# Moving a third of the taps of a depthwise convolution, and the low weight halves, from VectorE to ScalarE and GpSimd

## Chip, cores and metric
The kernel runs on one core of a Trainium2 chip, with all engines of that core: TensorE (PE), VectorE (DVE), ScalarE (ACT), GpSimd (POOL) and the DMA queue of SyncE (SP). The metric is the device time of one execution in microseconds. Inputs are float32, 512 tokens of width 1024.

## The reference
Two pre-norm residual layers. The even layer has a Conformer convolution beside differential attention, the odd layer a gated DeltaNet beside forgetting attention; each is followed by a SwiGLU block, and the end is an RMSNorm. The part that matters here is the even mixer:

```python
def even_mixer(h, ...):
    a_val, a_gate, q, k, v = _split(h @ w_in, [CONV_CH, CONV_CH, DIFF_QK, DIFF_QK, DIFF_V])
    u = a_val * jax.nn.sigmoid(a_gate)
    u = causal_depthwise_conv(u, conv_w) + conv_b   # 31 taps, 512 channels
    u = jax.nn.silu(layer_norm(u, ln_w, ln_b))
    q = partial_rotary(q...); k = partial_rotary(k...)
    o = diff_attention(q, k, v, lam)
    o = rms_norm(o, subln_w) * (1.0 - lambda_init)
    return jnp.concatenate([u, o.reshape(B_, S, DIFF_V)], axis=-1)
```

## The kernel before
Activations are held transposed: channels on the 128 partitions, 512 tokens along the free axis. A float32 product is made of three f32r products of a high and a low half, so each weight tile (128 x 1024 float32, 512 KB) takes this way: SP loads it into one of two buffers `raw`; ACT writes its high half (`hi(t)`, L544) and another engine the rest, raw minus high (`lo(t)`), into one of four slots of `wring`; PE uses it (24 matmuls) and sets `tile_used`. SP loads tile t+2 when hi(t) and lo(t) are done; hi(t) and lo(t) wait until tile t-4 has been used. In the even mixer `lo` is DVE's (L881). POOL has a `lo` of its own (L455), which it uses in the output projections and in the odd mixer.

The order of the even mixer is written out by hand in `even_order()`; each engine walks the same list and takes its own items:

- `val_gate` c = 0 to 3: two weight tiles each (0 to 7). DVE evacuates value and gate (L971), ACT takes the sigmoid, DVE writes the gated chunk c of 128 channels to `upad` (L974).
- `v` 0 to 3: tiles 8 to 11. `v_evac` copies the four values out (L1023).
- `qk`, eight query/key tiles (12 to 19), each in four parts, between which PE does other items. `qk_evac` is DVE's evacuation (L1026), `rope` the rotary product on PE and three DVE instructions (L985 to L988).
- 16 units of differential attention (head, block of 128 queries): `diff_s` scores on PE, `diff_m` maximum on DVE (L994) and exponentials on ACT (L609), `diff_w` combination on DVE (L1000 to L1005), `diff_t` transposes on PE and copy on ACT. The first five units are interleaved with query/key tiles 3 to 7.
- From unit 8 on the layer norm of the convolution (`ln_...`), which begins with POOL adding the four chunks.

The convolution is done tap by tap on DVE: for each of the four chunks one tensor_scalar (L946, tap 0 with the bias) and 30 scalar_tensor_tensor (L949), `cacc = upad shifted x weight + cacc`. They are put between the other DVE items by `pump(n)`, which issues the next n taps, in turns over the first two unfinished chunks that are there: 2 and `TAPS_VAL` in each val_gate, `TAPS_V` after each v, `TAPS_QK` after query/key tiles 0 and 2, one before each `rope`, `TAPS_UNIT` in each of the first five units.

The odd mixer has a short convolution of four taps over 12 chunks, on DVE: one tensor_scalar (L1117) and three scalar_tensor_tensor (L1119) for each chunk, while POOL writes low weight halves (L455).

## Time and profile before
| | |
|---|---|
| three runs, median (lowest, highest) | 1451.31 us (1448.43, 1455.08) |
| the profiled execution: its time, its span | 1448.43 us, 1446.6 us |
| PE, DVE, ACT, POOL busy, of the span | 1328.6, 724.4, 478.5, 174.3 us (92%, 50%, 33%, 12%) |
| L949, the fused taps | 120 instructions, 82.8 us |

Busy time of an engine is the time in which one of its instructions ran; an instruction that is held up after its start is counted as busy. The chain of waits is followed back from the last instruction: at each step to what released it, or to the instruction before it on its engine. A row of the timeline merges neighbours of one kind (x9 is nine of them) and gives in brackets how long the engine had been idle before and what ended that.

### The profile page before, as it was taken

The numbers are of one execution on the slowest core, as the hardware profiler recorded it, in microseconds if no ns is written. First come the engines' busy times: TensorE is split into PE (matmuls) and PEld (weight loads), VectorE is DVE, ScalarE is ACT, GpSimd is POOL, SyncE is SP. The second block draws the span as 40 slices with busy tenths as digits, with TensorE's granted clock in tenths as the row PEclk, the third lists the DMA queues.
The fourth block names the chain that finished last, engine by engine and source line by source line (L and its number), as shares of the span: only waits on it lengthen the run. The fifth ranks groups of instructions, "written<-read, shape, count | busy, mean of one in ns | idle before, by whom it ended". The sixth has DMA issues, their size and how long they took to land.

```text
span 1446.6 us, 16892 instructions
## 1 busy us (share of the span) xinstructions
PE 1328.6 (92%) x6250; PEld 1080.9 (75%) x6250; DVE 724.4 (50%) x991; ACT 478.5 (33%) x693; POOL 174.3 (12%) x103
## 2 busy tenths in 40 slices
PE   6886777899999999998998999987999999999995
PEld 4664445788888888886886888875788888888884
DVE  5898874454544442227874315355454544442223
ACT  4221234543333332214344322444343333332211
POOL 3000011410000000002423233210410000000005
PEclk9997887999999999999999999999999999999997
DMA  5221100123232232331221111100123232232221
GB/s 187 86 79 54 44 29 1 48 83 103 87 109 94 87 106 98 101 101 59 88 73 44 59 58 44 59 1 0 46 85 103 87 109 94 87 106 97 101 72 58
DMA packets 30718, 109.60 MB, mean 76 GB/s; under 512 B 3410, under 2 KB 3666, under 8 KB 30674
## 3 DMA queue, kind: packets, MB, share of 16 engines
q1 hardware_dynamic: 30674, 108.99, 22.5%
q8 instruction: 31, 0.51, 0.1%
q14 instruction: 13, 0.11, 0.0%
HBM read 106.88 MB, written 2.10 MB: 75 GB/s over the span
## 4 chain that ended last, share of the span: by engine, by line
PE 78%; DVE 16%; ACT 3%; issue 2%; POOL 1%; DMA 0%; DVEq 0%; SPq 0%; POOLq 0%; ACTq 0%
PE PS L1273 76%; DVE cacc L949 5%; DVE wring L881 2%; DVE hbuf L824 1%; DVE hbuf L1119 1%; ACT wring L544 1%; PE PS L1607 1%; DVE amax L994 1%; DVE HH L828 1%; POOL ssq L469 1%; PE PS L1349 0%; ACT pbuf L609 0%; DVE xT L842 0%; DVE qk L988 0%; DVE outT L1267 0%
## 5 line engine op out<-in xcount | busy, mean ns | idle before, releaser
L1273 PE MATMUL PS<-HH,wring 128*128 128x512 f32 x3096 | 747.5, 400 | 21.4 <-DVE wring L881 12.1
L1273 PEld LDWEIGHTS PS<-HH,wring 128*128 128x128 f32 x3096 | 585.8, 192 | 151.4 <-issue 20.9
L1273 PE MATMUL PS<-AA,wring 128*128 (+1 forms) x1440 | 328.2, 390 | 4.4 <-DVE AA L1010 2.8
L1273 PEld LDWEIGHTS PS<-AA,wring 128*128 128x128 f32 x1440 | 269.9, 188 | 61.9 <-DVE AA L1010 3.6
L852 DVE TENSOR_TENSOR ubuf<-PS,rstd 128x512 f32<-128x512 f32 x44 | 30.4, 691 | 198.1 <-PE PS L1273 198.1
L455 POOL TENSOR_TENSOR wring<-raw,wring 128x1024 fp32r<-128x1024 f32 x37 | 93.1, 2519 | 283.7 <-ACT wring L544 280.8
L874 DVE TENSOR_TENSOR wring<-raw,wring 128x1024 fp32r<-128x1024 f32 x36 | 44.1, 1226 | 149.6 <-ACT wring L589 149.6
L544 ACT ACTIVATE wring<-raw 128x1024 fp32r<-128x1024 f32 x73 | 76.7, 1053 | 122.7 <-PE PS L1273 81.2
L861 DVE TENSOR_TENSOR wring<-raw,wring 128x1024 fp32r<-128x1024 f32 x88 | 107.5, 1222 | 0.9 <-ACT wring L581 0.4
L466 POOL TENSOR_TENSOR ssq<-sqb 128x512 f32<-128x512 f32 x5 | 7.9, 1576 | 712.4 <-ACT sqb L557 712.4
L576 ACT ACTIVATE AA<-ubuf 128x512 f32 x44 | 27.9, 633 | 198.2 <-DVE ubuf L859 198.2
L581 ACT ACTIVATE wring<-raw 128x1024 fp32r<-128x1024 f32 x88 | 92.0, 1045 | 1.1 <-DMA raw<-w_stream 1.1
L589 ACT ACTIVATE wring<-raw 128x1024 fp32r<-128x1024 f32 x36 | 38.2, 1061 | 155.5 <-PE PS L1273 152.0
L949 DVE SCALAR_TENSOR_TENSOR cacc<-upad,vec,cacc 128x512 f32<-128x512 f32 x120 | 82.8, 745 | 0.5
L734 ACT ACTIVATE G<-PS 128x512 f32<-128x512 f32 x60 | 35.7, 595 | 105.2 <-PE PS L1607 52.7
L570 ACT ACTIVATE gbuf<-gbuf 128x512 f32<-128x512 f32 x44 | 27.8, 632 | 108.4 <-DVE gbuf L852 108.4
L1273 PE MATMUL PS<-wring,HH 128*128 128x512 f32 x192 | 51.2, 416 | 6.1 <-DVE hbuf L971 6.0
L881 DVE TENSOR_TENSOR wring<-raw,wring 128x1024 fp32r<-128x1024 f32 x36 | 45.5, 1278 | 20.9 <-ACT wring L544 20.8
L842 DVE TENSOR_TENSOR xT<-xT,PS 128x512 f32<-128x512 f32 x32 | 21.9, 683 | 59.5 <-PE PS L1273 59.5
L852 DVE TENSOR_TENSOR gbuf<-PS,rstd 128x512 f32<-128x512 f32 x44 | 30.4, 691 | 38.5 <-PE PS L1273 38.1
L1177 DVE COPY_PREDICATED G<-consts,PS 128x512 f32<-128x512 int32 x24 | 17.8, 741 | 63.6 <-PE PS L1273 63.6
L1273 PEld LDWEIGHTS PS<-wring,HH 128*128 128x128 f32 x192 | 36.8, 199 | 14.1 <-DVE hbuf L971 6.5
(232 smaller groups left out, 1132.7 us busy)
## 6 DMA issues: line engine op xcount, KB each, us to landing
raw<-w_stream SPq DMA_DIRECT2D x197, 512.0 KB, 3.2
xT<-x_t SPq DMA_DIRECT2D x4, 512.0 KB, 6.1
out_t<-outT SPq DMA_DIRECT2D x8, 256.0 KB, 2.1
rope<-rope_const SPq DMA_DIRECT2D x1, 576.0 KB, 4.4
consts<-shape_const SPq DMA_DIRECT2D x1, 576.0 KB, 5.8
consts<-shape_const SPq DMA_DIRECT2D x1, 192.0 KB, 7.0
vec<-vectors SPq DMA_DIRECT2D x1, 115.0 KB, 2.0
rowv<-row SPq DMA_DIRECT2D x1, 0.0 KB
```

The source lines that it names most:

```text
L455: nc.gpsimd.tensor_tensor(wring[:, t % RING, 1], raw[:, t % RAW], wring[:, t % RING, 0].bitcast(f32), ALU.subtract).then_inc(lo_ready[t % ...
L544: nc.scalar.activation(wring[:, t % RING, 0], raw[:, t % RAW], ACT.Copy).then_inc(hi_ready[t % RING], 1)
L576: nc.scalar.activation(AA[:, bass.ds(r * 2 + c, 1), 0].rearrange("p a b -> p (a b)"), ubuf[:, c], ACT.Copy).then_inc(sem("ffn_hi"), 1)
L581: nc.scalar.activation(wring[:, t % RING, 0], raw[:, t % RAW], ACT.Copy).then_inc(hi_ready[t % RING], 1)
L589: nc.scalar.activation(wring[:, t % RING, 0], raw[:, t % RAW], ACT.Copy).then_inc(hi_ready[t % RING], 1)
L734: nc.scalar.activation(out, hd(bank), func, **kw).then_inc(gdn_act[st], 1)
L852: V.tensor_tensor(buf[:, c], PS[:, 2 * c + u], rstd[:], ALU.mult).then_inc(evacuated, 1)
L861: V.tensor_tensor(wring[:, t % RING, 1], raw[:, t % RAW], wring[:, t % RING, 0].bitcast(f32), ALU.subtract).then_inc(lo_ready[t % RING], 1)
L874: V.tensor_tensor(wring[:, t % RING, 1], raw[:, t % RAW], wring[:, t % RING, 0].bitcast(f32), ALU.subtract).then_inc(lo_ready[t % RING], 1)
L881: V.tensor_tensor(wring[:, t % RING, 1], raw[:, t % RAW], wring[:, t % RING, 0].bitcast(f32), ALU.subtract).then_inc(lo_ready[t % RING], 1)
L949: ins = V.scalar_tensor_tensor(cacc[:, c], upad[:, c, k:k + S], vcol(V_CONVW + TAPS * c + k), cacc[:, c], ALU.mult, ALU.add)
L1273: return nc.tensor.matmul(out, lhsT, rhs, start=start, stop=stop)
```

## The change
1. Of the 124 taps, 39 leave DVE: taps 0 to 7 of chunk 2 and all 31 of chunk 3. ACT multiplies the shifted chunk by the weight into a ring `prod` of eight buffers (tap 0 of each goes with its bias straight to `cacc`), and POOL adds `prod` to `cacc`. They are a new item, `shared_taps`, two after each `v` and four after part 1 of each query/key tile. Semaphores `tap_product` (ACT to POOL) and `conv_added` (POOL to itself, to ACT for the ring, to DVE ahead of its tap 8 of chunk 2, and to POOL's first addition of the layer norm) go with it.
2. The low halves of tiles 4 to 23 (20 of them), written by DVE in `val_gate`, `v` and `qk_evac`, are written by POOL at the same items.
3. DVE's taps are fewer per item: 6, 5, 4, 5, 4 in place of 9, 8, 7, 7, 6.

```diff
--- before.py
+++ after.py
@@ -68,7 +68,10 @@
 OUT_DVE = 5
 
 
-TAPS_VAL, TAPS_V, TAPS_QK, TAPS_UNIT, TAPS_LATE = 9, 8, 7, 7, 6
+SHARED = 8
+PROD = 8
+POOL_TAPS_V, POOL_TAPS = 2, 4
+TAPS_VAL, TAPS_V, TAPS_QK, TAPS_UNIT, TAPS_LATE = 6, 5, 4, 5, 4
 LN_FROM = 8
 LAG = 6
 FILL_STEPS = 75
@@ -136,7 +139,16 @@
                      ("sub_lo", 0), ("sub_lo", 1), ("sub_lo", 2), ("conv_silu", 0), ("sub_mul", 3)]
     order += [("conv_lo", c) for c in range(4)] + [("sub_hi", 3), ("sub_lo", 3)]
 
-    return [item for item in order if item]
+    out, m = [], 0
+    for item in order:
+        if item:
+            out.append(item)
+            n = POOL_TAPS_V if item[0] == "v" else POOL_TAPS if item[0] == "qk" and item[1][1] == 1 else 0
+            if n and m < SHARED + TAPS:
+                out.append(("shared_taps", (m, min(m + n, SHARED + TAPS))))
+                m = min(m + n, SHARED + TAPS)
+    assert m == SHARED + TAPS
+    return out
 
 
 def fox_order():
@@ -302,7 +314,7 @@
     pbuf, q = at("pbuf", [2, 2, S], f32, q)
     wbuf, q = at("wbuf", [2, S], f32, q)
     assert q <= at_A + 4 * 2 * S * 4
-    prod, _ = at("prod", [2, S], f32, at_A + 4 * 2 * S * 4)
+    prod, _ = at("prod", [PROD, S], f32, at_A + 4 * 2 * S * 4)
     q = at_H
     oT, q = at("oT", [H, S], f32, q)
     osq, q = at("osq", [H, S], f32, q)
@@ -361,6 +373,14 @@
 
     def vcol(n):
         return vec[:, n:n + 1]
+
+    def shared_tap(m):
+
+        return (2, m) if m < SHARED else (3, m - SHARED)
+
+    def added(m):
+
+        return m if m < SHARED else m - 1
 
     sems = {}
 
@@ -472,10 +492,29 @@
             add_squares(0, n)
         nc.gpsimd.memset(upad[:, :, 0:TAPS - 1], 0.0).then_inc(sem("pad_zero"), 1)
 
+        def add_taps(m0, m1):
+            for m in range(m0, m1):
+                c, k = shared_tap(m)
+                if k:
+                    pool.wait_ge(sem("tap_product"), m + 1)
+                    if k > 1:
+                        pool.wait_ge(sem("conv_added"), added(m) - 1)
+                    nc.gpsimd.tensor_tensor(cacc[:, c], cacc[:, c], prod[:, m % PROD], ALU.add).then_inc(sem("conv_added"), 1)
+
         for kind, a in even_order():
-            if kind == "ln_add":
-
-                pool.wait_ge(sem("conv_done"), 4)
+            if kind == "val_gate":
+                lo(2 * a + RING)
+                lo(2 * a + 1 + RING)
+            elif kind == "v":
+                lo(8 + a + RING)
+            elif kind == "qk_evac":
+                lo(12 + a + RING)
+            elif kind == "shared_taps":
+                add_taps(*a)
+            elif kind == "ln_add":
+
+                pool.wait_ge(sem("conv_done"), 3)
+                pool.wait_ge(sem("conv_added"), added(SHARED + TAPS - 1))
                 for c in range(1, 4):
                     if c > 1:
                         pool.wait_ge(sem("ln_chunks"), c - 1)
@@ -620,11 +659,28 @@
                                  PS[:, bank, 0:(i + 1) * P].rearrange("p (j c) -> p j c", c=P),
                                  ACT.Copy).then_inc(sem(sem_c), 1)
 
+        def multiply_taps(m0, m1):
+
+            for m in range(m0, m1):
+                c, k = shared_tap(m)
+                if k == 0:
+                    act.wait_ge(sem("gated"), c - 1)
+                if m > PROD:
+                    act.wait_ge(sem("conv_added"), added(m - PROD))
+                w = vcol(V_CONVW + TAPS * c + k)
+                if k == 0:
+                    ins = nc.scalar.activation(cacc[:, c], upad[:, c, 0:S], ACT.Identity, bias=vcol(V_CONVB + c), scale=w)
+                else:
+                    ins = nc.scalar.activation(prod[:, m % PROD], upad[:, c, k:k + S], ACT.Copy, scale=w)
+                ins.then_inc(sem("tap_product"), 1)
+
         for kind, a in even_order():
             if kind == "qk" and a == (0, 0):
                 act.wait_ge(sem("masks_loaded"), 16)
                 nc.scalar.activation(mask16[:, 0], ident, ACT.Copy).then_inc(sem("mask16"), 1)
                 nc.scalar.activation(mask16[:, 1], cmask, ACT.Copy).then_inc(sem("mask16"), 1)
+            if kind == "shared_taps":
+                multiply_taps(*a)
             if kind == "val_gate":
                 hi(2 * a + RING)
                 hi(2 * a + 1 + RING)
@@ -931,10 +987,10 @@
         def taps():
 
 
-            tap, count = [0] * 4, [0] * 4
+            tap, count = [0, 0, SHARED], [0] * 3
             turn = 0
             while True:
-                open_ = [c for c in range(gated[0]) if tap[c] < TAPS][:2]
+                open_ = [c for c in range(min(gated[0], 3)) if tap[c] < TAPS][:2]
                 if not open_:
                     yield False
                     continue
@@ -945,7 +1001,10 @@
                 if k == 0:
                     ins = V.tensor_scalar(cacc[:, c], upad[:, c, 0:S], vcol(V_CONVW + TAPS * c), vcol(V_CONVB + c), ALU.mult, ALU.add)
                 else:
-                    dve.wait_ge(dchain, count[c])
+                    if count[c]:
+                        dve.wait_ge(dchain, count[c])
+                    else:
+                        dve.wait_ge(sem("conv_added"), added(SHARED - 1))
                     ins = V.scalar_tensor_tensor(cacc[:, c], upad[:, c, k:k + S], vcol(V_CONVW + TAPS * c + k), cacc[:, c],
                                                  ALU.mult, ALU.add)
                 if k < TAPS - 1:
@@ -971,10 +1030,12 @@
                 V.tensor_tensor(buf[:, c % 2], PS[:, (2 * c + m) % 4], rstd[:], ALU.mult).then_inc(evacuated, 1)
             pump(2 if c else 0)
             dve.wait_ge(sem("gate_sig"), c + 1)
-            link(V.tensor_tensor(upad[:, c, TAPS - 1:], hbuf[:, c % 2], sqb[:, c % 2], ALU.mult))
+            ins = V.tensor_tensor(upad[:, c, TAPS - 1:], hbuf[:, c % 2], sqb[:, c % 2], ALU.mult)
+            if c < 2:
+                link(ins)
+            else:
+                ins.then_inc(sem("gated"), 1)
             gated[0] += 1
-            lo(2 * c + RING)
-            lo(2 * c + 1 + RING)
             pump(TAPS_VAL)
 
         def rope_finish(j):
@@ -1015,8 +1076,6 @@
                 val_gate(a)
             elif kind == "taps":
                 pump(a)
-            elif kind == "v":
-                lo(8 + a + RING)
             elif kind == "v_evac":
                 dve.wait_ge(tile_used, 12)
                 for b in range(NB):
@@ -1025,7 +1084,6 @@
                 dve.wait_ge(tile_used, 12 + a + 1)
                 V.scalar_tensor_tensor(hbuf[:, a % 2], PS[:, QK_BANK[a]], 1.0 if a % 2 else SC_DIFF, rstd[:],
                                        ALU.mult, ALU.mult).then_inc(evacuated, 1)
-                lo(12 + a + RING)
             elif kind == "rope":
                 rope_finish(a)
             elif kind == "diff_m":
```

## Rows read from the trace of the kernel before

**Rows 1.** Windows: length; busy of PE, PEld, DVE, ACT, POOL; PEclk; DMA share, GB/s.
```profile
42.00:76.00 34.00, 26.19 (x111) 20.52 (x110) 33.44 (x47) 7.75 (x9) 0.00 (x0) 0.98 0.28 93
76.00:115.00 39.00, 29.77 (x120) 24.04 (x119) 38.97 (x57) 6.34 (x8) 0.00 (x0) 0.85 0.24 81
115.00:132.00 17.00, 15.18 (x58) 10.36 (x59) 13.66 (x20) 3.62 (x8) 0.00 (x0) 0.88 0.18 63
132.00:198.00 66.00, 48.31 (x172) 30.91 (x171) 56.57 (x92) 12.71 (x33) 2.68 (x3) 0.84 0.12 40
```

**Rows 2.** Chain of waits, 42 to 198 us: by line; a piece (start, us).
```profile
by line: DVE cacc L949 49.4%; DVE wring L881 13.6%; PE PS L1273 6.8%; issue 4.5%; DVE amax L994 3.0%; ACT pbuf L609 2.7%; DVE qk L988 2.7%; ACT wring L544 2.5%; DVE qk L985 2.4%; DVE sqb L986 2.4%; DVE upad L974 1.8%; DVE vtk L1023 1.7%; DV
...
80.39 5.96 DVE cacc L949 x9
```

**Rows 3.** Groups of the vector engine, 42 to 198 us: busy, mean, idle.
```profile
L949 DVE SCALAR_TENSOR_TENSOR cacc<-upad,vec,cacc 128x512 f32<-128x512 f32 x120 | 82.8, 745 | 0.5
L881 DVE TENSOR_TENSOR wring<-raw,wring 128x1024 fp32r<-128x1024 f32 x19 | 22.9, 1220 | 6.9 <-ACT wring L544 6.8
L1026 DVE SCALAR_TENSOR_TENSOR hbuf<-PS,rstd 128x512 f32<-128x512 f32 x8 | 5.5, 683 | 1.2 <-PE PS L1273 1.2
...
L986 DVE TENSOR_TENSOR sqb<-PS,rope 128x512 f32<-128x512 f32 x7 | 4.8, 683 | 0.0
...
L946 DVE TENSOR_SCALAR cacc<-upad,vec 128x512 f32<-128x512 f32 x4 | 2.2, 538 | 0.0
```

**Rows 4.** Timeline of PE: start, us, idle before it and releaser.
```profile
75.52 5.06 PE L1273 MATMUL PS<-wring,HH 128*128 128x512 f32 x11 [6.02 <-DVE hbuf L971]
...
115.06 2.04 PE L1273 MATMUL PS<-hbuf,rope 128*128 128x512 f32 x2 [9.30 <-DVE hbuf L1026]
```

**Rows 5.** Line L1026: min/median/max ns, first and last start.
```profile
L1026 DVE SCALAR_TENSOR_TENSOR hbuf<-PS,rstd x8: 674/681/692, 114.2 to 197.5; 128x512 f32<-128x512 f32 x8
```

**Rows 6.** Timeline of the vector engine, 691 to 765 us, the short convolution.
```profile
691.30 2.33 DVE L1119 SCALAR_TENSOR_TENSOR hbuf<-cin,vec,hbuf 128x512 f32<-128x512 f32 x3
...
694.98 4.34 DVE L1119 SCALAR_TENSOR_TENSOR hbuf<-cin,vec,hbuf 128x512 f32<-128x512 f32 x3
...
759.85 4.47 DVE L1119 SCALAR_TENSOR_TENSOR hbuf<-cin,vec,hbuf 128x512 f32<-128x512 f32 x3
```

**Rows 7.** Timeline of GpSimd in four places.
```profile
195.17 1.27 POOL L482 TENSOR_TENSOR prod<-cacc 128x512 f32<-128x512 f32 x1 [171.52 <-DVE cacc L949]
...
273.17 4.95 POOL L455 TENSOR_TENSOR wring<-raw,wring 128x1024 fp32r<-128x1024 f32 x2 [49.76 <-ACT wring L544]
...
307.77 1.62 POOL L469 TENSOR_TENSOR ssq<-ssq,sqb 128x512 f32<-128x512 f32 x1 [3.82 <-ACT sqb L557]
...
695.98 2.79 POOL L455 TENSOR_TENSOR wring<-raw,wring 128x1024 fp32r<-128x1024 f32 x1 [6.16 <-ACT wring L544]
```

**Rows 8.** Timeline of the vector engine beside GpSimd in three other places.
```profile
13.27 0.49 DVE L824 TENSOR_SCALAR hbuf<-xT,vec 128x512 f32<-128x512 f32 x1
...
14.46 1.32 DVE L824 TENSOR_SCALAR hbuf<-xT,vec 128x512 f32<-128x512 f32 x1
...
273.09 0.68 DVE L842 TENSOR_TENSOR xT<-xT,PS 128x512 f32<-128x512 f32 x1
273.81 2.05 DVE L824 TENSOR_SCALAR hbuf<-xT,vec 128x512 f32<-128x512 f32 x1
...
306.41 0.69 DVE L828 TENSOR_TENSOR HH<-hbuf,HH 128x512 fp32r<-128x512 f32 x1
307.01 1.22 DVE L881 TENSOR_TENSOR wring<-raw,wring 128x1024 fp32r<-128x1024 f32 x1
308.15 1.78 DVE L828 TENSOR_TENSOR HH<-hbuf,HH 128x512 fp32r<-128x512 f32 x1
```

**Rows 9.** Tile cacc: an activation, min/median/max ns.
```profile
L656 ACT ACTIVATE ytmp<-cacc,vec x4: 800/800/817, 259.2 to 261.4; 128x512 f32<-128x512 f32 x4
```

**Rows 10.** Groups of the scalar engine, 42 to 198 us.
```profile
L544 ACT ACTIVATE wring<-raw 128x1024 fp32r<-128x1024 f32 x17 | 18.0, 1059 | 61.3 <-PE PS L1273 35.1 <-DMA raw<-w_stream 26.2
```

## Prediction

> **What bounds the kernel now.** I read the page first, for the span and the engines, then the stretches around the convolution, the chain of waits, the groups of the vector engine, and last the timeline wherever the vector engine and GpSimd work at the same time. The profiled execution took 1448.43 us, with a span of 1446.6. All that the change touches lies between 42 us, where the first gated channel chunk is written, and 198 us, where the last query/key tile is evacuated. There the vector engine (DVE) is busy 33.4 + 39.0 + 13.7 + 56.6 = 142.6 us of 156, and TensorE (PE) 26.2 + 29.8 + 15.2 + 48.3 = 119.4 us [rows 1]. From 76 to 115 us DVE has no free time at all, and the chain of waits gives half of the stretch to the taps (L949) and another 14% to the lo halves (L881) [rows 2]. PE pays for it: it stands 6.0 us for the evacuation of the last value/gate tile and 9.3 us for that of the first query tile [rows 4]. GpSimd (POOL) does nothing before 132 us, ScalarE (ACT) is busy a fifth of the time [rows 1]. So this stretch is bound by DVE in program order, and what lengthens or shortens DVE's work here moves the end almost one to one. What comes after 198 us is the same in both kernels, and I let it move with the stretch.
>
> **What goes from DVE.** Chunk 2 loses its first 8 taps and chunk 3 all 31: two of these are plain tensor_scalar, 37 the fused form. In a row of taps one starts every 5.96 / 9 = 0.66 us [rows 2] (its 745 ns overlap the next [rows 3]), so this is 37 x 0.66 + 2 x 0.46 (538 ns [rows 3] less the same 0.08 of overlap) = 25.4 us. The 20 lo halves of tiles 4 to 23 leave too: 20 x 1.14 (1220 ns less 0.08 [rows 3]) = 22.8 us. Together 48.2 us. If nothing were paid for it, DVE would need 94.4 us of the stretch and PE's 119.4 would bound it.
>
> **What ACT gets.** 39 multiplications with a scale from a vector. The nearest row, an ACTIVATE of the same size with scale and bias from vectors, is 800 ns [rows 9]; the bare one of twice the size takes 1059 [rows 10]. So 39 x 0.6 to 0.8 = 23 to 31 us, on an engine with 156 - 30.4 us free [rows 1]. In its order they sit after a hi conversion and ahead of the transposed copy and the exponentials of a unit, 4 at a time: 2.4 to 3.2 us, in time in which ACT waits for DVE's maximum. I take nothing for them. Without that cover each of the eight groups would cost up to 3 us, 24 in all; the product ring of 8 also lets ACT wait for POOL's additions of two groups before, which comes to the same.
>
> **What POOL gets.** 37 additions (taps 1 to 7 and 1 to 30) at 1.27 us each, as its only one of this form beside an idle DVE [rows 7], 47 us, and 20 lo halves at about 2.4 (the two at 273 us took 4.95 [rows 7]), 48 us: 95 us of 156. By itself that fits, and the four-slot ring of weights leaves a tile's lo half three tiles of PE work (over 15 us) before PE asks for it. DMAs: none is added, but SP's load of tile t+2 waits for lo(t), which now stands behind up to 4 additions in POOL's queue (about 5 us). With a DMA share of 0.24 or less from 76 us on [rows 1] I take nothing for it. Two waits are new to DVE and to the chunk's order: its tap 8 of chunk 2 waits for POOL's seven additions, with the rotary work queued behind it. DVE comes to that tap only after 56 others, in the query/key tiles, and POOL's seven are in the value tiles before; I take nothing, and a microsecond or two if POOL is late.
>
> **What POOL's work costs DVE.** This is the term that decides. Later in the same kernel DVE runs exactly this fused form, three in a chain. Undisturbed the three take 2.33 us; with one lo half on POOL beside them they take 4.34 [rows 6, 7]. Of the twelve such triples between 691 and 768 us nine are of the long kind; the last of these took 4.47 [rows 6]. So one lo half stops DVE for 2.0 to 2.2 us. With an addition on POOL a DVE subtraction of two SBUF operands grows from 0.69 to 1.78 us [rows 8]: 1.1 us; a tensor_scalar grew from 0.49 to 1.32, 0.83 us [rows 8]. That subtraction stood right behind another DVE instruction, and POOL, waiting since 307.77, still got in between [rows 7, 8]: where both have work, they take turns. A DVE instruction that takes one operand from PSUM kept its 0.68 us at 273.09 beside POOL's lo half, while the tensor_scalar after it grew to 2.05, by 1.6 [rows 8]. So evacuations, PSUM products and maxima run beside POOL; taps, the gated product, two thirds of the rotary work and the combinations do not. The Trainium skill (SBUF — State Buffer, "Who interferes with whom") has this as an exclusive lock between the two engines, held for the whole instruction. The rows agree in kind. By a whole instruction of POOL's the sum below would be 12 us higher (95 us in place of 83); the growth in the rows is smaller, and I go by the rows.
>
> Full price: 20 x 2.1 + 37 x 1.1 = 82.7 us on DVE against 48.2 saved, so +34.5 us if nothing of it is covered. Cover is DVE's idle time, 156 - 142.6 = 13.4 us, and its instructions that read PSUM: two groups of 5.5 and 4.8 us [rows 3], ten other evacuations of the same size (7) and seven maxima (an estimate of 5), some 22 us. With all of it used: 34.5 - 35.4 = -1. With the cheapest growth seen (0.83 us for an addition, 1.6 for a lo half) and all cover, 62.6 - 48.2 - 35.4 = -21. I walk through the stages to see how much cover is really met:
>
> - 42 to 76 us: 9 taps and 6 lo halves go (6.0 + 6.8 = 12.8 us); lo halves 4 to 11 come on POOL, 8 x 2.1 = 16.8, of which some 3 fall beside the wait for the sigmoid and the evacuations. +1. PE's wait of 6.0 us stays.
> - 76 us to the first query evacuation at 114.2 [rows 5]: 15 taps and 6 lo halves go (16.7 us). DVE has 28 taps in a row and POOL has always something ready (lo 12 to 16, and ACT and POOL run ahead of PE with chunk 2's seven additions and seven of chunk 3), so they take turns: 5 x 2.1 + 14 x 1.1 = 25.9. +9. PE's wait of 9.3 us grows to 18.
> - 115 to 132 us: two tiles, DVE partly idle; one lo half and four additions fall beside the rotary work. +2 (0 to 5).
> - 132 to 198 us: five more lo halves and 19 additions, 10.5 + 20.9 = 31.4; 12 taps and 5 lo halves go, 13.6; of the 17.8 left, 9.4 is met by DVE's idle time in this stage (66 - 56.6 [rows 1]; 6.8 of the idle in the whole stretch was DVE waiting for ACT ahead of its own lo halves [rows 3], which falls away) and some 2 by PSUM instructions, since the additions come right behind a lo half, when DVE has rotary work and taps, and not when it has its maxima. +6. The last of the eight evacuations, at 197.5 now [rows 5], comes near 216.
>
> Sum: 1 + 9 + 2 + 6 = +18 us; 1448.4 + 18 = 1466.4. The three runs have a median of 1451.3, 3 us above the profiled one; I forecast 1467.
>
> **The rivals.**
> - POOL's work is hidden and DVE's 48 us are gained. For it: POOL idle until 132 us [rows 1], DVE busy 91% of the stretch. Then PE's 119.4 us bound the stretch, 36.6 us less, 1412 us; half hidden, about 1430. Against it: nine of twelve triples. It decides from the point where less than 48 of the 83 us fall into time that DVE needs; by my count it is 67.
> - A draw: the growths are the small ones and most PSUM instructions are met, 62.6 - 48.2 - 13.4 = +1, 1444 to 1456.
> - PE becomes the second loser: longer waits let its granted clock fall. From 76 to 115 us, with the waits, it was 0.85, at 132 to 198 0.84, against 0.98 before 76 [rows 1]; at 1.2 GHz a tile of 24 products is twice as long. If the five units lose another 2 to 3 us each, that is +10 to 15 on top, 1477 to 1485.
> - ACT in the way: its groups of multiplications delay exponentials, up to 24 us more, the same place in the range.
>
> **How the numbers follow.** Under 0.5% (7 us) a measurement of this kernel can't tell from no change. The stall of DVE with the clock as now (1456 to 1477): 0.50. With PE or ACT on top (1477 to 1495): 0.16. A draw: 0.14. Hidden: 0.20. So slower 0.66, same 0.14, faster 0.20. The likeliest case alone spans 1456 to 1477; the range that leaves out 2 in 10 goes from 1440 to 1488.
>
> **What would show it.** Right: fused taps of 745 ns with a share at 1.8 (an addition) and 2.9 us (a lo half), a mean well over 1 us; DVE's busy time in the stretch as long as before or longer although its instructions are 59 fewer; the first query evacuation near 124 us and not before 115; the last well after 198; PE's wait before the first rotary product longer than 9.3 us. ACT's multiplications near 0.7 us with no waits behind them. Wrong: taps of 745 ns throughout; the last query/key evacuation before 198 us; a chain of waits that leads from 42 to 198 us mainly over PE; or POOL waiting in DVE's stead, its additions at 1.9 us and DVE's undisturbed.

## The result, and the profile after

The changed kernel took 1462.54 us (median of ten runs, 1458.36 to 1468.19), the kernel before 1451.71 us on the same chips (ten runs, 1448.16 to 1455.73). The ratio is 1.007, with a 95% interval of 1.005 to 1.0091: slower, by 10.8 us. The profiled execution took 1462.84 us, with a span of 1459.7.

The stretches of the changed kernel, with the columns of [rows 1]:

```profile
42.00:76.00 34.00, 24.87 (x110) 20.27 (x108) 33.57 (x30) 7.29 (x9) 18.13 (x7) 0.93 0.36 124
76.00:115.00 39.00, 36.20 (x146) 29.04 (x146) 28.79 (x39) 15.60 (x23) 30.27 (x11) 0.93 0.13 44
115.00:132.00 17.00, 7.54 (x27) 4.47 (x28) 12.25 (x11) 6.54 (x12) 16.28 (x10) 0.60 0.16 55
132.00:198.00 66.00, 43.25 (x155) 28.41 (x154) 63.95 (x71) 21.65 (x46) 41.50 (x25) 0.81 0.12 40
```

VectorE (DVE) issues 151 instructions here, 65 fewer than in [rows 1] (59 by the change; the rest lies in the slower order, which has not come as far by 198 us), and is busy 138.6 us where it had been busy 142.6. So the instructions left take longer. But the stages differ from the forecast: from 76 to 115 us TensorE (PE) is busy 36.2 us, 6.4 more than before, and DVE is idle for 10.2 us; from 115 to 132 us PE works 7.5 us where it had worked 15.2. Something was gained and given back. The groups by line, 42 to 198 us, say what grew:

```profile
L1008 DVE SCALAR_TENSOR_TENSOR cacc<-upad,vec,cacc 128x512 f32<-128x512 f32 x83 | 88.6, 1111 | 5.4 <-POOL cacc L502 4.9
...
L475 POOL TENSOR_TENSOR wring<-raw,wring 128x1024 fp32r<-128x1024 f32 x17 | 55.5, 3274 | 41.0 <-ACT wring L583 41.0
L502 POOL TENSOR_TENSOR cacc<-cacc,prod 128x512 f32<-128x512 f32 x34 | 51.6, 1519 | 3.3
...
L674 ACT ACTIVATE prod<-upad,vec 128x512 f32<-128x512 f32 x35 | 23.0, 712 | 3.2 <-POOL cacc L502 3.2
```

The 83 fused taps on DVE (L1008) take 88.6 us; 120 took 82.8 before [rows 3]. GpSimd's (POOL's) low halves (L475) average 3.27 us, though one takes 2.4 to 2.5 undisturbed. And there is a wait that was not there, 4.9 us of DVE for POOL's additions (L502). The evacuations of the query tiles, to be held against [rows 5]:

```profile
L1085 DVE SCALAR_TENSOR_TENSOR hbuf<-PS,rstd x8: 673/680/692, 104.9 to 204.9; 128x512 f32<-128x512 f32 x8
```

The first comes 9.4 us earlier than before, the last 7.4 us later. The timeline of DVE shows where that turns:

```profile
78.72 17.30 DVE L1008 SCALAR_TENSOR_TENSOR cacc<-upad,vec,cacc 128x512 f32<-128x512 f32 x26
99.42 2.73 DVE L1082 TENSOR_SCALAR vtk<-PS,rtok 128x512 f32<-128x512 f32 x4 [3.39 <-PE PS L1331]
104.86 0.69 DVE L1085 SCALAR_TENSOR_TENSOR hbuf<-PS,rstd 128x512 f32<-128x512 f32 x1 [2.71 <-PE PS L1331]
105.47 5.43 DVE L1008 SCALAR_TENSOR_TENSOR cacc<-upad,vec,cacc 128x512 f32<-128x512 f32 x3
115.80 3.42 DVE L1008 SCALAR_TENSOR_TENSOR cacc<-upad,vec,cacc 128x512 f32<-128x512 f32 x2 [4.91 <-POOL cacc L502]
119.14 1.75 DVE L1046 TENSOR_TENSOR qk<-hbuf,rope 128x512 f32<-128x512 f32 x1
120.81 0.68 DVE L1047 TENSOR_TENSOR sqb<-PS,rope 128x512 f32<-128x512 f32 x1
121.52 2.12 DVE L1049 TENSOR_TENSOR qk<-qk,sqb 128x512 f32<-128x512 f32 x1
123.56 0.68 DVE L1085 SCALAR_TENSOR_TENSOR hbuf<-PS,rstd 128x512 f32<-128x512 f32 x1
```

And that of POOL beside it:

```profile
84.30 13.98 POOL L475 TENSOR_TENSOR wring<-raw,wring 128x1024 fp32r<-128x1024 f32 x1 [11.82 <-ACT wring L583]
98.25 1.28 POOL L502 TENSOR_TENSOR cacc<-cacc,prod 128x512 f32<-128x512 f32 x1
...
106.88 3.46 POOL L502 TENSOR_TENSOR cacc<-cacc,prod 128x512 f32<-128x512 f32 x2
110.30 2.83 POOL L475 TENSOR_TENSOR wring<-raw,wring 128x1024 fp32r<-128x1024 f32 x1
113.10 7.23 POOL L502 TENSOR_TENSOR cacc<-cacc,prod 128x512 f32<-128x512 f32 x5
```

From 78.72 to 96.02 us DVE runs 26 taps without a hold-up, 0.66 us each. POOL's low half, begun at 84.30, ends at 98.28, 2.26 us after the last of those taps: it did its work only when DVE had stopped. No turns were taken. The additions, whose products ACT had written from 85 us on, began at 98.25. DVE came to the ninth tap of chunk 2, its own first there, at 110.9, found them unfinished and stood 4.91 us; now turns were taken, and the five taps around it took 8.85 us where undisturbed ones take 3.3. Between the first two evacuations lie 18.7 us; it had been 9.0. PE stood for 11.86 us of it, before the rotary product of the second query tile:

```profile
106.02 1.02 PE L1331 MATMUL PS<-hbuf,rope 128*128 128x512 f32 x2
106.48 6.05 PE L1331 MATMUL PS<-HH,wring 128*128 128x512 f32 x24
124.39 2.05 PE L1331 MATMUL PS<-hbuf,rope 128*128 128x512 f32 x2 [11.86 <-DVE hbuf L1085]
```

It is the successor of the 9.30 us in [rows 4], one tile later.

### The profile page after: what moved, and what is told of

It is laid out like the page before. It is cut to its first block, busy times and chain, and to the rows that moved or that the text cites. A ratio compares the mean times of both kernels' runs of the same rounds, so it can differ in the third digit from the quotient of the medians.

```text
span 1459.7 us, 16982 instructions
## 1 busy us (share of the span) xinstructions
PE 1332.5 (91%) x6250; PEld 1085.1 (74%) x6250; DVE 728.7 (50%) x932; ACT 502.3 (34%) x732; POOL 293.3 (20%) x160
## 3 DMA queue, kind: packets, MB, share of 16 engines
q1 hardware_dynamic: 30674, 108.99, 21.6%
## 4 chain that ended last, share of the span: by engine, by line
PE 79%; DVE 13%; issue 3%; ACT 2%; POOL 2%; DMA 0%; DVEq 0%; SPq 0%; POOLq 0%; ACTq 0%
PE PS L1331 78%; DVE cacc L1008 4%; DVE hbuf L880 1%; DVE qk L1046 1%; PE PS L1665 1%; POOL cacc L502 1%; DVE HH L884 1%; DVE amax L1055 1%; PE PS L1407 1%; POOL ssq L489 1%; DVE qk L1049 1%; DVE hbuf L1177 0%; ACT wring L583 0%; DMA xT<-x_t 0%; DVE xT L898 0%
## 5 line engine op out<-in xcount | busy, mean ns | idle before, releaser
L1331 PE MATMUL PS<-HH,wring 128*128 128x512 f32 x3096 | 746.4, 399 | 20.1 <-DVE wring L937 12.2
L475 POOL TENSOR_TENSOR wring<-raw,wring 128x1024 fp32r<-128x1024 f32 x57 | 155.8, 2739 | 352.8 <-ACT wring L583 352.8
L930 DVE TENSOR_TENSOR wring<-raw,wring 128x1024 fp32r<-128x1024 f32 x36 | 44.1, 1226 | 149.6 <-ACT wring L628 149.6
L917 DVE TENSOR_TENSOR wring<-raw,wring 128x1024 fp32r<-128x1024 f32 x88 | 107.5, 1221 | 0.9 <-ACT wring L620 0.4
L583 ACT ACTIVATE wring<-raw 128x1024 fp32r<-128x1024 f32 x73 | 76.4, 1052 | 84.3 <-PE PS L1331 54.2
L1008 DVE SCALAR_TENSOR_TENSOR cacc<-upad,vec,cacc 128x512 f32<-128x512 f32 x83 | 88.6, 1111 | 5.4 <-POOL cacc L502 4.9
L502 POOL TENSOR_TENSOR cacc<-cacc,prod 128x512 f32<-128x512 f32 x37 | 56.2, 1519 | 3.6
L489 POOL TENSOR_TENSOR ssq<-ssq,sqb 128x512 f32<-128x512 f32 x30 | 42.5, 1415 | 44.0 <-ACT sqb L596 43.0
```

The source lines that it names most:

```text
L475: nc.gpsimd.tensor_tensor(wring[:, t % RING, 1], raw[:, t % RAW], wring[:, t % RING, 0].bitcast(f32), ALU.subtract).then_inc(lo_ready[t % ...
L489: nc.gpsimd.tensor_tensor(ssq[:], ssq[:], sqb[:, n % 2], ALU.add).then_inc(ssq_done, 1)
L502: nc.gpsimd.tensor_tensor(cacc[:, c], cacc[:, c], prod[:, m % PROD], ALU.add).then_inc(sem("conv_added"), 1)
L583: nc.scalar.activation(wring[:, t % RING, 0], raw[:, t % RAW], ACT.Copy).then_inc(hi_ready[t % RING], 1)
L917: V.tensor_tensor(wring[:, t % RING, 1], raw[:, t % RAW], wring[:, t % RING, 0].bitcast(f32), ALU.subtract).then_inc(lo_ready[t % RING], 1)
L930: V.tensor_tensor(wring[:, t % RING, 1], raw[:, t % RAW], wring[:, t % RING, 0].bitcast(f32), ALU.subtract).then_inc(lo_ready[t % RING], 1)
```

## The experiments

The questions were four: is it the contention between DVE and POOL that eats the 48 us, or the new order with its waits; which of the two kinds of work on POOL costs what; what kept POOL out for 14 us; and can DVE be taken out of the contention. All kernels below start from the changed kernel, except where another is named.

**Both kinds of POOL's work made small (pool_small).** Instructions, waits and semaphores stay, but POOL's subtraction and addition touch 16 columns only, so the output lacks most of the low parts of the weights of tiles 4 to 23 and most of 37 taps. `lo_small` stands for `lo` in `val_gate`, `v` and `qk_evac`; "..." marks lines left out.

```diff
+        def lo_small(t):
+            ...
+            nc.gpsimd.tensor_tensor(wring[:, t % RING, 1, 0:16], raw[:, t % RAW, 0:16], wring[:, t % RING, 0, 0:16].bitcast(f32), ALU.subtract)
-                    nc.gpsimd.tensor_tensor(cacc[:, c], cacc[:, c], prod[:, m % PROD], ALU.add)
+                    nc.gpsimd.tensor_tensor(cacc[:, c, 0:16], cacc[:, c, 0:16], prod[:, m % PROD, 0:16], ALU.add)
```

> The changed kernel, but POOL's 37 additions and its 20 low halves of the even mixer work on 16 columns only (the rest of the sums and of the low halves is left out); every item, wait and order stays. Theory A (POOL's work costs DVE through the port that both use): the 48 us that left DVE are now really gained and PE bounds the stretch, 1412 to 1425 us. Rival B (what is lost lies in the order, in ACT's multiplications or in PE's own waits): the time stays near the changed kernel's, above 1445.

Measured: 1412.76 us (1405.49 to 1416.46), ratio 0.9715 (0.9677 to 0.9754). The taps are undisturbed, and the last query evacuation comes at 155.0:

```profile
L1016 DVE SCALAR_TENSOR_TENSOR cacc<-upad,vec,cacc x83: 741/746/781, 45.0 to 149.2; 128x512 f32<-128x512 f32 x83
```

So with the order and all waits as changed, the kernel is 39 us faster than before if POOL's instructions are short, and the length of POOL's instructions costs 49.8 us. The order, ACT's 39 products and the waits are not what makes it slow.

**One kind made small at a time (adds_small, lo_small).** In the first, only the additions touch 16 columns (37 taps are mostly missing from the output), in the second only the low halves (the low weight parts are mostly missing).

> The changed kernel with only the 37 additions cut to 16 columns (most of the sums is left out), the low halves whole. Theory A: DVE gets back up to 37 x 1.1 us less what was covered, and the wait for the seven additions goes; fused taps stay long only beside low halves; 1425 to 1442 us. If the low halves alone made the loss: above 1450.

> The changed kernel with only the 20 low halves on POOL cut to 16 columns (most of each is left out), the additions whole. With adds_small at 1438.5 and both cut at 1412.8: if the two prices simply add up, the low halves cost 26 us and the additions 24, and this takes 1436 to 1440. If POOL's additions come mainly late because the low half before them waits (theory C), it takes less, 1420 to 1432.

Measured: additions small 1438.53 us (1434.72 to 1443.85), ratio 0.9921 (0.9892 to 0.995); low halves small 1432.3 us (1424.16 to 1436.15), ratio 0.9849 (0.9809 to 0.9889). Against 1462.5 the additions cost 24.0 us and the low halves 30.2. The two nearly add up to the 49.8 (54.2); the expectation for the second had 1436 to 1440 us for prices that simply add and 1420 to 1432 for additions that come late behind a waiting low half, and 1432.3 lies on the edge of the latter and decides little. Per instruction that is 0.65 us of the kernel's time for an addition and 1.5 for a low half.

**One part of the change at a time (taps_only, lo_only).** First the taps only, with the low halves back on DVE; then, made from the kernel before, the low halves only, with all 124 taps on DVE. Of each edit one engine's part is shown; the other engine gains or loses the same `lo` items.

```diff
 taps only, POOL:
-            if kind == "val_gate":
-                lo(2 * a + RING)
-            ...
 low halves only, DVE of the kernel before:
-            lo(2 * c + RING)
-            lo(2 * c + 1 + RING)
```

> Part 1 alone: taps shared with ACT and POOL, low halves back on DVE. Theory A (price per addition 1.1 us wherever DVE has a gap): 25 us leave DVE, up to 41 come back, some 13 of them covered: 1446 to 1460. Theory C (the loss is that POOL comes late, since its first low half waited 12 us for a run of taps and the additions behind it): without low halves POOL isn't late, 1428 to 1440.

> Part 2 alone: the 20 low halves on POOL, all 124 taps on DVE with the old counts. Theory A: 23 us leave DVE, 20 x 2.1 = 42 come back less what is covered; 1450 to 1465. Theory C: DVE runs 41 taps without a gap from about 78 us; POOL gets none of its low halves in before 105 us and PE waits for tile 12 for some 8 us, with fused taps at 745 ns in that run; the same range, told apart by the length of the first low half after 80 us (over 15 us by C, under 4 by A with turns).

Measured: taps only 1466.14 us (1465.14 to 1467.19), ratio 1.0101 (1.0083 to 1.012); low halves only 1468.6 us (1465.29 to 1474.15), ratio 1.0128 (1.0101 to 1.0155). Each half of the change alone is as slow as both together or slower, and slower than any theory on record had it (6 us above 1460, 4 above 1465): less of the price is covered than was estimated. With the taps only, DVE's low halves cut its taps into fives, and POOL takes its turns from 79 us on. The first row is of DVE, the second of POOL:

```profile
93.30 8.51 DVE L1001 SCALAR_TENSOR_TENSOR cacc<-upad,vec,cacc 128x512 f32<-128x512 f32 x5
```
```profile
92.04 16.43 POOL L502 TENSOR_TENSOR cacc<-cacc,prod 128x512 f32<-128x512 f32 x9 [2.33 <-ACT prod L667]
```

Five taps in 8.51 us are 1.70 each, 1.04 above the undisturbed 0.66. With the low halves only, the first query evacuation comes at 125.5; the first low half after 80 us took 8.9 us, between the "over 15" and "under 4" of the two theories.

**Without the wait for seven additions (chunk3).** `SHARED = 0`: POOL and ACT take chunk 3 alone, and chunk 2 is all DVE's, so DVE waits for none of POOL's additions (DVE has 8 taps more, POOL 7 additions fewer).

> The changed kernel, but only chunk 3 is shared (31 taps on ACT and POOL, 93 on DVE), so that DVE never waits for POOL's additions. DVE has 8 taps more (5.3 us), POOL 7 additions less (7.7 us of price, most of it uncovered), and the wait of 4.9 us goes. Theory C (lateness costs): 1452 to 1458, 5 us or more under the changed kernel. Theory A (only the price on the port): 1459 to 1463.

Measured: 1464.0 us (1462.03 to 1470.35), ratio 1.009 (1.0063 to 1.0117). The second query evacuation comes at 118.38, 5.2 us earlier than in the changed kernel, but the fourth at 152.69 beside 152.54, and the last at 202.9. So the wait's 4.9 us aren't what the kernel loses by: the theory that made the wait the cause expected 1452 to 1458 us, and is out (the other had 1459 to 1463, 1 us too low). The lock-out is here as well: a low half took 14.34 us from 83.96 us on. That the 8 taps more on DVE, in the units, are what gave the 5 us back is the likely reading, not a shown one.

**Gaps between the taps (one_chunk).** DVE takes its taps from one chunk at a time, so that each waits for the one before it. With that its own taps cost more, about 0.79 us each.

```diff
-                open_ = [c for c in range(min(gated[0], 3)) if tap[c] < TAPS][:2]
+                open_ = [c for c in range(min(gated[0], 3)) if tap[c] < TAPS][:1]
```

> The changed kernel, but DVE does the taps of one chunk after another and not of two in turns, so that every tap waits for the one before it. Theory D (POOL gets the port only when DVE leaves a gap or POOL held it last): the first low half after 80 us takes under 4 us and not 14, POOL's seven additions are done in time, and DVE's wait for them (4.9 us) goes, but in the value tiles DVE is held up as the prediction had it; the taps start 0.79 us apart at best. 1465 to 1485 us. Rival (the run of taps isn't what kept POOL out): the low half keeps its 14 us.

Measured: 1474.29 us (1469.36 to 1475.29), ratio 1.0149 (1.0132 to 1.0166). POOL first, then DVE:

```profile
88.37 2.45 POOL L475 TENSOR_TENSOR wring<-raw,wring 128x1024 fp32r<-128x1024 f32 x1 [12.14 <-ACT wring L583]
90.78 1.47 POOL L502 TENSOR_TENSOR cacc<-cacc,prod 128x512 f32<-128x512 f32 x1
```
```profile
91.14 32.92 DVE L1008 SCALAR_TENSOR_TENSOR cacc<-upad,vec,cacc 128x512 f32<-128x512 f32 x18
```

The low half that took 13.98 us takes 2.45; DVE pays in its stead, 1.83 us for each of the next 18 taps, and its first query evacuation comes at 126.6. There is no wait for additions any more.

**How long a run keeps POOL out (lo_last, lo_turn3).** Two more, made from low halves only. There the run over chunks 0 and 1 kept POOL out from 90.89 to about 97.4 us, but a later one over chunks 1 and 2, with taps as close, let it in after 0.4 us. The first kernel turns over the last two unfinished chunks once there are four, the second over three chunks in place of two.

```diff
-                open_ = [c for c in range(gated[0]) if tap[c] < TAPS][:2]
+                open_ = [c for c in range(gated[0]) if tap[c] < TAPS]
+                open_ = open_[-2:] if gated[0] == 4 else open_[:2]
 and in the other one:
+                open_ = [c for c in range(gated[0]) if tap[c] < TAPS][:3]
```

> lo_only with one difference: once all four chunks are there (85 us), VectorE takes its taps in turns from the last two unfinished chunks (2 and 3) and not from the first two (0 and 1). Open question: in lo_only a run of taps over chunks 0 and 1 kept GpSimd out from 90.9 to 97.4 us, and the same kind of run over chunks 1 and 2, with starts every 0.66 us too, let it in after 0.4 us. Theory that a run without gaps keeps it out by itself: it stays out here until the run ends or changes its chunks, some 10 us or more, and the first low half of about 90 us takes over 10 us. Theory that it hangs on which buffers the run touches: the low half of about 90 us gets in at once, 2.4 to 2.9 us long, the following ones too, and each stops VectorE for 2.1 us: first query evacuation 124 to 130 us, time 1464 to 1475 us.

> lo_only with turns over three unfinished chunks in place of two, so that the tap on which the next one of its chunk depends is three instructions back. Theory that GpSimd gets in through the small wait of a tap for the one two before it: here there is none, the run keeps GpSimd out wherever three chunks are open (from 70 us on), the low halves of 75 to 120 us take over 8 us each and TensorE waits for them, first query evacuation before 120 us. Theory that the spacing of dependent taps plays no part: the low halves behave as in lo_only (one long wait of 5 to 10 us, then 2.4 to 2.9 us each), first query evacuation 122 to 128 us, time 1462 to 1475 us. In either case the taps start every 0.66 us where GpSimd is quiet.

Measured: last two 1470.23 us (1466.98 to 1473.55), ratio 1.0117 (1.0092 to 1.0142); three in turns 1463.31 us (1462.97 to 1467.74), ratio 1.0069 (1.0053 to 1.0086). Of the first kernel, DVE and then POOL:

```profile
87.99 25.92 DVE L957 SCALAR_TENSOR_TENSOR cacc<-upad,vec,cacc 128x512 f32<-128x512 f32 x39
113.83 2.72 DVE L1027 TENSOR_SCALAR vtk<-PS,rtok 128x512 f32<-128x512 f32 x4
124.17 0.69 DVE L1030 SCALAR_TENSOR_TENSOR hbuf<-PS,rstd 128x512 f32<-128x512 f32 x1 [7.62 <-PE PS L1276]
```
```profile
92.78 25.66 POOL L455 TENSOR_TENSOR wring<-raw,wring 128x1024 fp32r<-128x1024 f32 x2 [14.06 <-ACT wring L551]
```

39 taps ran at 0.66 us each over chunks 2 and 3, and POOL, with a low half begun at 92.78, got nothing done until they ended: two low halves took 25.66 us. The theory of the buffers, by which chunks 2 and 3 would have let it in at once, is out, though the first evacuation (124.2) and the time lie inside what it had forecast. DVE's taps are now undisturbed, but PE waits 8.4 us for the low half, and DVE waits 7.6 us for PE instead: the time is the same as with turns. With three in turns POOL's pair took 22.63 us from 90.38, and it got in when the first tap of the last chunk, a tensor_scalar at 108.22, cut the run; in low halves only it was such a first tap too, at 97.43. The expectation for it was met in the first, long hold, missed in the low halves after it (2.5 to 2.8 us, not over 8) and by 0.9 us in the evacuation (120.9, not before 120). So POOL gets into a close run of three chunks in turn as well (at 115.17). What sets the entries at 104.37 and 112.66 us of low halves only apart is taken up in the last section.

**DVE's operand taken out of SBUF (psum_acc).** In the changed kernel, the sums of chunks 0 and 1 stay in two idle PSUM banks until their last tap, so each of their taps reads one operand from SBUF and one from PSUM. Chunk 2 begins after both, PE waits for them before the scores that need the banks, and the counts of taps are 7, 6, 4, 4, 4.

```diff
+        def acc(c):
+            return PS[:, 6 + c] if c < 2 else cacc[:, c]
 ...
-                    ins = V.scalar_tensor_tensor(cacc[:, c], upad[:, c, k:k + S], vcol(V_CONVW + TAPS * c + k), cacc[:, c],
+                    ins = V.scalar_tensor_tensor(acc(c) if k < TAPS - 1 else cacc[:, c], upad[:, c, k:k + S], vcol(V_CONVW + TAPS * c + k), acc(c),
 ...
+                if a == 1:
+                    pe.wait_ge(sem("conv_done"), 2)
```

> The changed kernel, but DVE's sums of chunks 0 and 1 stand in PSUM (banks 6 and 7, free until the second scores) up to their last tap, so that 60 of DVE's 83 fused taps read one operand from SBUF and one from PSUM; one chunk pair first, then chunk 2; two taps more per value/gate tile pair, one more per value tile and one less per unit. Theory A (DVE instructions with one SBUF operand run beside POOL): up to 125 us POOL's work costs DVE almost nothing and those taps stay at 0.75 us, the first low half after 80 us takes under 3 us; 1430 to 1442 us, under both kernels. Rival (POOL holds up any DVE instruction, or the taps get longer with PSUM): no gain, 1455 or more.

Measured: 1434.81 us (1431.4 to 1441.02), ratio 0.9883 (0.9851 to 0.9915): 27.7 us less than the changed kernel and 17 less than the one before. It computes the whole reference and beats both. DVE and POOL of the same place:

```profile
70.04 16.54 DVE L1011 SCALAR_TENSOR_TENSOR PS<-upad,vec,PS 128x512 f32<-128x512 f32 x25
```
```profile
72.66 2.40 POOL L475 TENSOR_TENSOR wring<-raw,wring 128x1024 fp32r<-128x1024 f32 x1 [3.09 <-ACT wring L583]
75.02 1.29 POOL L502 TENSOR_TENSOR cacc<-cacc,prod 128x512 f32<-128x512 f32 x1
78.10 2.41 POOL L475 TENSOR_TENSOR wring<-raw,wring 128x1024 fp32r<-128x1024 f32 x1 [1.78 <-ACT wring L583]
80.47 2.73 POOL L502 TENSOR_TENSOR cacc<-cacc,prod 128x512 f32<-128x512 f32 x2
```

25 taps at 0.66 us each, and in the same time low halves at 2.4 and additions at 1.3 us: neither holds up the other. Most of these taps also write to PSUM, so it could be the writing that counts. It isn't: a last tap reads PSUM and writes SBUF, and it kept its 0.73 us in the middle of POOL's additions:

```profile
86.50 0.73 DVE L1011 SCALAR_TENSOR_TENSOR cacc<-upad,vec,PS 128x512 f32<-128x512 f32 x1
85.91 2.73 POOL L502 TENSOR_TENSOR cacc<-cacc,prod 128x512 f32<-128x512 f32 x2
```

The taps and rotary products that still read two operands from SBUF go on paying, in the groups of DVE from 42 to 210 us:

```profile
L1011 DVE SCALAR_TENSOR_TENSOR PS<-upad,vec,PS 128x512 f32<-128x512 f32 x58 | 40.1, 747 | 0.5
L1011 DVE SCALAR_TENSOR_TENSOR cacc<-upad,vec,cacc 128x512 f32<-128x512 f32 x23 | 31.2, 1356 | 0.4
L1049 DVE TENSOR_TENSOR qk<-hbuf,rope 128x512 f32<-128x512 f32 x8 | 15.0, 1877 | 1.8 <-PE PS L1334 1.8
```

**The same sums in PSUM without POOL (psum_before), and with the low halves only (psum_lo).** The edit of the last kernel, made in the kernel before and in low halves only, with their own counts.

> The kernel before, with the sums of chunks 0 and 1 kept in PSUM until their last tap and nothing moved to GpSimd or ScalarE. Contention theory (PSUM sums helped the changed kernel only because a tap with one operand from PSUM runs beside GpSimd): nothing runs on GpSimd here between 42 and 195 us, so nothing is gained: taps 740 to 750 ns, first query evacuation 112 to 116 us, time 1447 to 1456 us, ratio 0.997 to 1.003. Rival (a sum in PSUM is cheaper for VectorE by itself, or shortens its chain of dependent taps): the 62 taps gain 0.1 us or more each, the first query evacuation comes before 109 us, time below 1445 us. Second rival (it is dearer by itself, by the wait that TensorE gets before its second scores): above 1457 us.

> Low halves on GpSimd, all 124 taps on VectorE as in lo_only, with the sums of chunks 0 and 1 in PSUM until their last tap. Contention theory: the low halves that fall beside chunks 0 and 1 (about 10 of 20, until some 95 us) cost VectorE nothing and don't wait for it (1.3 to 2.5 us each, no start later than 3 us after its high half), so 22.8 us leave VectorE and 10 x 2.1 = 21 less idle time and PSUM cover (about 12) come back: 12 to 15 us less than the kernel before on VectorE, first query evacuation 98 to 106 us, time 1436 to 1446 us. Rival (what psum_acc won came from the 39 taps that left VectorE, and low halves on GpSimd cost as much as before): 1460 to 1470 us, as lo_only had 1468.6.

Measured: without POOL 1456.12 us (1450.45 to 1460.42), ratio 1.003 (1.0017 to 1.0043); with low halves 1447.0 us (1445.54 to 1449.55), ratio 0.9966 (0.9953 to 0.9979). Without POOL the sums in PSUM gain nothing and cost 0.3%. A first tap takes 0.81 us there, not 0.54, and chunk 2 begins later; that these make the 0.3% is not shown. (Its first query evacuation, at 119.1, lies outside the 112 to 116 expected, and the time 0.1 us above its 1447 to 1456, but 3.3 of its 4.9 us were there before the first tap: the first gated product began at 45.47 in place of 42.14.) So the gain of the kernels above is the absence of contention and not a cheaper tap. With the low halves it is 21.6 us less than low halves only; the low halves beside the runs in PSUM took 2.35 to 2.6 us, with no hold. The first query evacuation came at 108.7, 3 us later than the latest expected, and the time 1 us above the range given.

## Why the prediction was right, and where it was not

**The outcome and the mechanism** were right: slower, by 10.8 us where 15.7 were forecast (1462.5 for 1467.0), inside the likeliest case's 1456 to 1477. What eats the gain is DVE held up by POOL, which pool_small isolates and psum_acc with psum_before confirms.

**What goes from DVE (48.2 us)** was sized well. From the first gated chunk to the last query/key evacuation, of the kernel before, the changed one and pool_small (columns of [rows 1]):

```profile
42.14:197.55 155.41, 119.31 (x459) 85.69 (x457) 142.18 (x213) 29.86 (x53) 2.31 (x2) 0.88 0.19 65
42.14:204.90 162.76, 118.58 (x459) 86.54 (x457) 144.30 (x154) 53.57 (x92) 112.54 (x55) 0.84 0.18 62
43.69:154.95 111.26, 104.51 (x459) 78.43 (x457) 95.05 (x155) 53.02 (x92) 31.73 (x54) 1.00 0.25 86
```

With POOL's instructions short, DVE is busy 95.0 us (94.4 in the prediction). The hidden rival's 1412 us was met (1412.8), but in part by luck: the granted clock was 1.00, PE was busy 104.5 us and not 119.4, and the stretch got 44 us shorter where 36.6 were counted; by the first addition to the residual it was 37.1 us (234.9 for 272.0).

**The prices** held wherever turns are taken. An addition beside a tap costs 1.04 us (1.1 in the prediction). A rotary product beside a low half takes 2.91 us where it had taken 0.68, so 2.2 (2.0 to 2.2). Of the changed kernel, DVE, then POOL:

```profile
155.02 2.91 DVE L1046 TENSOR_TENSOR qk<-hbuf,rope 128x512 f32<-128x512 f32 x1
```
```profile
154.91 2.47 POOL L475 TENSOR_TENSOR wring<-raw,wring 128x1024 fp32r<-128x1024 f32 x1 [7.03 <-ACT wring L583]
```

One row was used for more than it shows: the instruction with a PSUM operand at 273.09 [rows 8] had begun before POOL's at 273.17 [rows 7], so it could not have been held up. That such instructions do run beside POOL is seen in the changed kernel, whose first query evacuation took 0.69 us at 104.86 inside this low half:

```profile
104.53 2.41 POOL L475 TENSOR_TENSOR wring<-raw,wring 128x1024 fp32r<-128x1024 f32 x1
```

**How much of the price was paid** was mis-sized. The full price was put at 82.7 us and by the walk through the stages about 66 were to be paid (48.2 + 18). DVE paid 49.3 (144.3 less 95.0 busy), and its idle time in the stretch grew by 5.2 (18.5 for 13.2), nearly all of it the wait of 4.9. How the 33 us that were not paid divide into idle time, PSUM reads and the 14 us in which POOL was locked out was not measured.

**The stages** against the sum. Starts of four evacuations, before and after, with the shift of each and the forecast shift up to there:

| | before | after | shift | forecast |
|---|---|---|---|---|
| last value/gate (L971, L1030) | 74.79 | 75.60 | +0.8 | +1 |
| first query (L1026, L1085) | 114.24 | 104.86 | -9.4 | +10 |
| third query/key | 132.24 | 133.59 | +1.4 | +12 |
| last query/key | 197.55 | 204.90 | +7.4 | +18 |

The first stage is right (+0.8 for +1; only PE's wait in it, which was to stay at 6.0 us, was 9.5) and so is the last, 132 to 198 us (+6.0 for +6). **The step that failed** is that of 76 us to the first query evacuation: "DVE has 28 taps in a row and POOL has always something ready [...], so they take turns", 25.9 us, +9. It came out at -10.2. That taps stand in a row is just what kept POOL out: in 17.3 us not one tap was held up. The rows it was read from ([rows 6 to 8]) were a chain of three dependent taps and a subtraction with another instruction ahead; none was a long run without gaps. one_chunk, in which the taps do have gaps, shows what the step described: first query evacuation 126.6 (forecast "near 124"), and 1474 us. Its own taps are slower too, so its 1474 is no clean price of the turns.

**The next step failed with it.** 115 to 132 us was put at +2, and the wait for seven additions at nothing, "a microsecond or two if POOL is late". POOL was late because it had been locked out (in one_chunk, without the lock-out, there is no such wait), and DVE came to the tap after 53 others, not 56. From the first to the third evacuation the shift is +10.7: the second tile alone has 4.9 us of waiting, 5.5 us of hold in five taps and 2.5 in the rotary work, less 3.1 for the low half and three taps that left DVE there. So the two errors, 19 us too dear and 9 too cheap, left the sum 11 us too high at 198 us, and 5 in the end. That the total came out right is in part luck.

**Whether the lock-out itself made the kernel slower** is not shown. chunk3, without the wait, gains nothing in the end; lo_last, with a lock-out nearly twice as long, takes what low halves only takes, and lo_turn3, whose first low half was held for 20.1 us, takes 5 us less. A likely reading, not a shown one: what DVE wins by it PE loses, since PE needs POOL's low halves as much as DVE's evacuations.

**Behind 198 us** I let the work move with the stretch. In the profiled pair, the first addition to the residual comes 9.2 us later (272.0 before, 281.2 after), where 7.4 came in; the one at 906.9 us is 8.3 late. The spans differ by 13.1 us and the medians by 10.8: the 2 to 5 us past the 8 lie within what single runs of one kernel differ by, and no place is named for them.

**The other rivals.** PE's clock: the granted 0.60 of 115 to 132 us stands for a stage in which PE had 7.5 us of work; from 132 to 198 us it was 0.81 against 0.84 [rows 1], and the stage cost no more than forecast. Over the whole stretch PE was busy 118.6 us, and 119.3 before. ACT in the way: its products took 712 ns (forecast 0.6 to 0.8) and waited 3.2 us in all for POOL. Neither came. The Trainium skill (SBUF — State Buffer, "Who interferes with whom") says that the shared ports are an exclusive lock, that the first to issue gets them for its whole instruction (written in that section of VectorE's two-port modes), that issue order decides who blocks, and that a VectorE instruction with at most one SBUF input does not contend. The turns after 98 us and the taps of psum_acc, which read one operand from SBUF and ran free, agree with that page. The hold of 13.98 us does not follow from it, since it spans 18 instructions of DVE and not the one that was under way.

**Of the signs named,** the mean tap of 1111 ns, the taps beside additions and low halves, DVE's busy time as long as before (144.3 us for 142.2, with 59 instructions fewer, up to the last evacuation), the late last evacuation and ACT's 712 ns were there. The first query evacuation was not: at 104.9 it met the sign that was to show the forecast wrong ("not before 115"), and PE's long wait came a tile later. The last evacuation came at 204.9, not 216.

## What to carry to other kernels

Before work is moved from VectorE to GpSimd, count for each VectorE instruction beside it how many operands it reads from SBUF: here the move would have freed 39 us of the kernel's time and contention took 50, and the same move with 60 of the taps reading their running sum from PSUM was worth 17 us. A price of contention read from short chains didn't hold here for a long run of instructions without gaps: there GpSimd was the one that stood, and whoever waited for GpSimd paid later. Follow the work that another engine owes through the whole stage before a new wait is put down at nothing.

## What the runs showed of the hardware that was not expected

A run of VectorE instructions with two SBUF operands each and no gaps (0.66 us apart) kept GpSimd out to its end: 13.98 us beside a run of 26 taps, 25.66 us for two low halves beside 39 taps. It is not a matter of the size of GpSimd's operation. In pool_small an operation on 16 columns, 0.22 us otherwise, stood as long and ended with the run (69.63 + 17.31 = 86.94 us):

```profile
73.74 13.28 POOL L483 TENSOR_TENSOR wring<-raw,wring 128x16 fp32r<-128x16 f32 x1 [5.21 <-ACT wring L591]
86.98 0.22 POOL L510 TENSOR_TENSOR cacc<-cacc,prod 128x16 f32<-128x16 f32 x1
```

Taps that wait for the one before them (0.79 us apart) let it in at once, and once GpSimd has work back to back, the two alternate one to one, a tap each 1.70 us beside additions. In two kernels a long hold ended at a tensor_scalar in the middle of a run (low halves only at 97.43 us, three in turns at 108.22; 2.63 and 2.57 us long).

But a close run does not always keep GpSimd out: in low halves only it got in at 104.37 and 112.66 us, in the middle of one. The single records of the traces show what these entries have in common. Count the fused taps that VectorE has begun one right behind the other, since the last hold-up or other instruction, at the moment at which GpSimd's operation begins. All eight long holds, one each in the changed kernel, pool_small, adds_small, lo_small, chunk3, lo_only, lo_last and lo_turn3, began during the seventh, eighth or ninth such tap. The two entries came during the third and the fourth, and every other operation of full size that got in beside such a run, in any of the traces, came before the fifth. During the fifth and sixth only 16-column operations came, at the last tap of a run, and they tell nothing. This is a regularity of these traces, not a tested cause: no run moved the arrival alone.
